# Prompt attention on one core: the values of a pair move between the second head's scores and its transposes

## The chip, the cores and the metric

The kernel runs on one NeuronCore of one Trainium2 chip. The metric is the device time of one execution in microseconds (us); the kernel before was timed three times, and the median of these runs is the number to compare with.

## What is computed

One inference step of a one-layer decoder with two groups of attention heads, for a prompt of 1024 positions and for eight short samples. The change touches the attention of the prompt alone. Cut to what matters there:

```python
def attend_block(t_pos, q_n, gates, q_f, cq, kw, vw, w_pos, kc, vc, c_end, ovl, ksb, vsb, kf, vf, ck, rel_bias):
    ...
    lc = jnp.einsum('bqgrd,bcgd->bgrqc', qg, kc).astype(jnp.float32) * scale + t5_bias_2d(dist_c, rel_bias)
    pc = masked_softmax(lc, dist_c >= 0)
    o_c = jnp.einsum('bgrqc,bcgd->bqgrd', pc.astype(vc.dtype), vc)
    ...
    ls = jnp.einsum('bqgrd,bgqmd->bgrqm', qg, ks_sel).astype(jnp.float32) * scale + bias_s.astype(jnp.float32)
    ps = masked_softmax(ls, (dist_s >= 0)[:, :, None])
    o_s = jnp.einsum('bgrqm,bgqmd->bqgrd', ps.astype(vs_sel.dtype), vs_sel)
    ...
    lw = jnp.einsum('bqgrd,bkgd->bgrqk', qg, kw).astype(jnp.float32) * scale + t5_bias_2d(dist_w, rel_bias)
    pw = masked_softmax(lw, valid_w)
    o_w = jnp.einsum('bgrqk,bkgd->bqgrd', pw.astype(vw.dtype), vw)
    ...
    lf = jnp.einsum('bqhd,bkhd->bhqk', q_f, kf).astype(jnp.float32) * scale + decay
    pf = masked_softmax(lf, k_pos[None, :] <= t_pos[:, None])
    o_f = jnp.einsum('bhqk,bkhd->bqhd', pf.astype(vf.dtype), vf).reshape(B, Q, FOX_HEADS * HEAD_DIM)
```

## The kernel before

The program has five stages one after the other: projections, the samples' attention, the prompt's attention (`build_c`, L1911 on), the output projection, and the feed-forward network. `build_c` is the stage of the change. In the profile its scores of the causal blocks start at 582 us and its last instruction ends at 957 us.

**Units, pairs, macros.** A unit is one softmax of 128 queries of one head (`unit_table`, L1626). Its kind is cmp, slc, win or fox. Two units, the two heads e = 0 and 1, make a pair `p`. For each of four head pairs hp and each of eight query tiles m there is a macro of three pairs: slc m, win m, fox m. The keys of a unit are n tiles of 128: n = m + 1 for slc, at most 5 for win, and 8 - m for fox, which takes its query tiles from the other end. One more pair, cmp of the next hp, stands between macro 4 and macro 5 of the first three head pairs. So there are 96 pairs with values and four of kind cmp.

**The way of a unit.** TensorE computes its scores into a slot of PSUM (`scores`, L2011; L2044 and L2045, both of type fp32r with 128-column weights). VectorE adds the bias and takes the maximum (`peak`, L2241). ScalarE takes the exponent (`exponent`, L2117, L2129) and counts `exp_done`. TensorE turns the probabilities in blocks of 128 x 128 (`turn`, L2048, L2053, fp32) into one of three banks of a ring, four blocks to an entry. ScalarE copies the entries out (`copies`, L2139), but VectorE copies the second entry of head 1 (L2289). At last TensorE multiplies the turned probabilities with the values (`values`, L2056, L2073 and L2080): fp32 matmuls on two halves of the array's columns, 64 wide each, one for either head, so that their weights have a shape that no other step of the loop has. An fp32 value product stands in the trace as two matmuls, so a pair of n tiles shows 4n of them, and slc pairs four more for cmp.

**Slots.** Four banks of PSUM hold scores. A unit with more than four tiles takes two banks, another one takes one (`slot_table`, L1707). Before it writes, `scores(u)` waits until the exponent of the unit that had its banks is done (L2102). For 50 of the second heads that is the unit two before, so the second head of the preceding pair; for the others it is an older one.

**Rounds.** Each engine has its order written out as a loop over rounds p. TensorE's is:

```python
for p in ROUNDS:
    for e in range(2):
        for u in pair_of(p + 1)[e:e + 1]:
            if SLOT_BEFORE[u] is not None:
                pe.wait_ge(exp_done, SLOT_BEFORE[u] + 1)
            scores(u)
        for u in pair_of(p)[e:e + 1]:
            pe.wait_ge(exp_done, u + 1)
            turn(u)
    if p - 2 in ENDS:
        natural(ENDS[p - 2])
    if p - 3 in ENDS:
        mix(ENDS[p - 3])
    if 0 <= p - 1 < NP:
        values(p - 1)
```

Written with S for scores, T for transposes, V for values and the head's number behind, a round is S0 T0 S1 T1 V, and its S belong to pair p + 1, its T to p, its V to p - 1. Four transposes of the finished macro (`natural`, L2084, L2088) stand ahead of V in a round of a win pair, two more (`mix`, L2091, L2095 and L2096) in that of a fox pair. Values of a cmp pair do nothing.

ScalarE's round (L2146 on) is: copies of head 0 of pair p, exponent of head 0 of p + 1, copies of head 1 of p, then in the round of a slc pair (or of cmp behind macro 4) the copy of the finished macro's sums `outT` (L2166), which waits until V of that round is done, and then the exponent of head 1 of p + 1. An engine works through its list in this order.

Of the kernel before, what the change touches and what calls it, by code (L numbers as in the profile page):

```python
# [1638 lines left out]
NP = NU // 2  # L1639
# [12 lines left out]
def key_tiles(m, kind):  # L1652

    if kind == "cmp":
        return 0, 4
    i = q_tile(m, kind)
    lo = max(0, i - WIN // P) if kind == "win" else 0
    return lo, i + 1 - lo
# [86 lines left out]
def pair_of(p):  # L1745

    return [2 * p, 2 * p + 1] if 0 <= p < NP else []
# [104 lines left out]
def fox_loads(hp):  # L1852

    return 128 * (hp // 2 + 1)
# [56 lines left out]
def build_c(nc, a, o, c, env, mixT, low, w_o, w_o_loaded, squares):  # L1911
# [13 lines left out]
    with ctx:  # L1925
# [33 lines left out]
        def query_of(macro, of):  # L1959
            hp, m = divmod(macro, QT)  # L1960
            if of == "nsa":
                return q_nsa[:, (hp + 1) % 2, :, m * P:(m + 1) * P], high_odd[:, 0] if macro % 2 else high_nsa
            i = q_tile(m, "fox")
            return q_fox[:, hp % 2, :, i * P:(i + 1) * P], high_odd[:, 1] if macro % 2 else high_fox

        def slot_of(u):
            hp, m, kind, e = UNITS[u]
            n = key_tiles(m, kind)[1] * P
            at = 512 * SLOT_BANK[u] + (512 - n // 2 if kind == "cmp" or n > 512 else 0)
            return slots[:, at:at + n]  # L1970
# [17 lines left out]
        with nc.Block() as block:  # L1988
# [19 lines left out]
            def _(pe):  # L2008
                pe.wait_ge(filled, 2)

                def scores(u):  # L2011
                    hp, m, kind, e = UNITS[u]
                    g = hp // 2
                    lo, n = key_tiles(m, kind)
                    slot = slots[:, 512 * SLOT_BANK[u]:]
                    if kind == "cmp":
                        if e == 0:
                            if hp == 0:
                                pe.wait_ge(kv_loaded, 192)
                            else:  # L2020
                                pe.wait_ge(q_loaded[hp % 2], 64 * ((hp + 1) // 2))
                        for j in range(4):
                            for par in range(2):
                                i = QT - 1 - 2 * j - par
                                part = slice(par * DH, (par + 1) * DH)
                                last = nc.tensor.matmul(slot[:, 256 + par * 256 + j * DH:256 + par * 256 + (j + 1) * DH],
                                                        q_nsa[part, (hp + 1) % 2, e, i * P:(i + 1) * P].bitcast(F32), k_cmp[part, g, :], start=True, stop=True)
                        last.then_inc(scored, 1)
                        return
                    if kind == "fox":  # L2030
                        if m == 0 and e == 0:
                            pe.wait_ge(fox_loaded[hp % 2], fox_loads(hp))
                        k = k_fox[:, hp % 2, e, :]
                    else:
                        k = (k_slc if kind == "slc" else k_win)[:, g, :]
                    of = "fox" if kind == "fox" else "nsa"
                    q_low, q_high = query_of(hp * QT + m, of)
                    if e == 0:
                        POOL.wait(pe, ("low", of, hp * QT + m))
                    dst = slot_of(u)  # L2040
                    w = n * P // 2 if n > 4 else n * P
                    for at in range(0, n * P, w):
                        keys = k[:, lo * P + at:lo * P + at + w]
                        nc.tensor.matmul(dst[:, at:at + w], q_high[:, e, :], keys, start=True, stop=False)  # L2044
                        last = nc.tensor.matmul(dst[:, at:at + w], q_low[:, e, :], keys, start=False, stop=True)  # L2045
                    last.then_inc(scored, 1)

                def turn(u):  # L2048
                    for g in entries_of(u):
                        _, at, n = ENTRIES[g]  # L2050
                        wait_place(pe, ("turn", g))
                        for j in range(n):
                            last = nc.tensor.transpose(place(("turn", g))[:, j * P:(j + 1) * P], probs[:, u % 4, (at + j) * P:(at + j + 1) * P], ident[:, :])  # L2053
                        last.then_inc(turned, 1)
# [43 lines left out]
# [3 lines that stand above are left out]
                            if SLOT_BEFORE[u] is not None:  # L2101
                                pe.wait_ge(exp_done, SLOT_BEFORE[u] + 1)  # L2102
                            scores(u)
                        for u in pair_of(p)[e:e + 1]:
                            pe.wait_ge(exp_done, u + 1)
                            turn(u)
                    if p - 2 in ENDS:
                        natural(ENDS[p - 2])
                    if p - 3 in ENDS:
                        mix(ENDS[p - 3])  # L2110
                    if 0 <= p - 1 < NP:
                        values(p - 1)

            @block.scalar
            def _(act):

                def exponent(u):  # L2117
                    hp, m, kind, e = UNITS[u]
                    n = key_tiles(m, kind)[1] * P
                    act.wait_ge(max_done, u + 1)  # L2120
                    if u >= 4:
                        act.wait_ge(turned, entries_of(u - 4)[-1] + 1)
                        if UNITS[u - 4][2] == "cmp":
                            STAT.wait(act, ("total", u - 4))
                    if kind == "cmp":
                        nc.scalar.activation(probs[:, u % 4, 0:n], slot_of(u), ACT.Exp).then_inc(exp_done, 1)
                    else:
                        at = 2 * KINDS.index(kind) + e
                        nc.scalar.activation(probs[:, u % 4, 0:n], slot_of(u), ACT.Exp, bias=neg_max[:, u % 4:u % 4 + 1], scale=-1.0 if turned_over(u) else 1.0,  # L2129
                                             accum_out=denom[:, m % 2, at:at + 1]).then_inc(exp_done, 1)  # L2130

                def copy(g):
                    u, at, n = ENTRIES[g]
                    hp, m, kind, e = UNITS[u]
                    act.wait_ge(turned, g + 1)
                    if u >= 4 and kind != "cmp" and UNITS[u - 4][2] != "cmp":
                        act.wait_ge(summed, summed_through((u - 4) // 2))
                    dst = cmpT[:, hp % 2, e, 0:n * P] if kind == "cmp" else probsT[:, u % 4, at * P:(at + n) * P]
                    nc.scalar.copy(dst, place(("turn", g))[:, 0:n * P]).then_inc(copied["A"], 1)  # L2139

                def copies(u):
                    for g in entries_of(u):
                        if ENTRY_ON[g] == "A":
                            copy(g)

                for p in ROUNDS:  # L2146
                    if p - 4 in ENDS:
                        macro = ENDS[p - 4]
                        hp, m = divmod(macro, QT)
                        src = place(("mix", macro))  # L2150
                        CLOSE_PE.wait(act, ("mix", macro))
                        nc.scalar.copy(mixT[:, hp, m * P:(m + 1) * P], src[:, 0:P])
                        i = q_tile(m, "fox")
                        CLOSE_ACT.done(nc.scalar.copy(mixT[:, H // 2 + hp, i * P:(i + 1) * P], src[:, P:2 * P]), ("mix", macro))
                    for u in pair_of(p)[:1]:
                        copies(u)
                    for u in pair_of(p + 1)[:1]:
                        exponent(u)
                    for u in pair_of(p)[1:]:
                        copies(u)  # L2160
                    if p - 1 in ENDS:
                        macro = ENDS[p - 1]
                        act.wait_ge(summed, summed_through(last_pair(macro)))
                        if macro:
                            CLOSE_PE.wait(act, ("natural", macro - 1))
                        CLOSE_ACT.done(nc.scalar.copy(outT[:, :, :].rearrange("p k n -> p (k n)"), outs), ("out", macro))  # L2166
                    for u in pair_of(p + 1)[1:]:
                        exponent(u)

# [1257 lines left out]
```

## Time and profile before

| | |
|---|---|
| median of three runs | 1823.34 us |
| lowest and highest | 1818.98 and 1825.59 us |
| time of the profiled execution | 1820.88 us |
| span of its instructions | 1819.2 us |
| busy over the span: PE (TensorE), DVE (VectorE), ACT (ScalarE) | 95%, 55%, 40% |
| mean granted TensorE clock | 0.98 |
| prompt attention, 582 to 957 us | 375 us |

The span runs from the first to the last instruction; 1.7 us of the execution's time lie outside of it. Matmuls are pipelined: one begins before the other's shown end, and their ends are modelled. So how long a run of matmuls holds the engine is read from start to start here. PE is the matmul row and PEld the row of weight loads. "idle before <-releaser" names what ended an engine's wait.

### The profile page before, as it was taken

The numbers are of one execution on the slowest core, as the hardware profiler recorded it, in microseconds if no ns is written. First come the engines' busy times: TensorE is split into PE (matmuls) and PEld (weight loads), VectorE is DVE, ScalarE is ACT, GpSimd is POOL, SyncE is SP. The second block draws the span as 40 slices with busy tenths as digits, with TensorE's granted clock in tenths as the row PEclk, the third lists the DMA queues.
The fourth block names the chain that finished last, engine by engine and source line by source line (L and its number), as shares of the span: only waits on it lengthen the run. The fifth ranks groups of instructions, "written<-read, shape, count | busy, mean of one in ns | idle before, by whom it ended". The sixth has DMA issues, their size and how long they took to land. (4 is left out here: it accounts for less than half of the span.)

```text
span 1819.2 us, 35393 instructions
## 1 busy us (share of the span) xinstructions
PE 1722.9 (95%) x13557; PEld 1577.7 (87%) x13557; DVE 1007.6 (55%) x1891; ACT 723.6 (40%) x1439; POOL 300.9 (17%) x629
## 2 busy tenths in 40 slices
PE   8999999799895999999998999999999999999998
PEld 7999998676573888888886879999999999999998
DVE  4533332124353666667665567766656664666665
ACT  5111010222231778676775642233333333344343
POOL 3000024410502434453530000000000000000000
PEclk9999999899996999999998999999999999999998
DMA  5548876645999103030202232222222225131112
GB/s 147 183 131 192 227 226 117 205 135 177 299 347 266 63 1 106 1 105 2 94 1 74 90 122 83 72 83 85 80 71 71 82 96 203 65 132 44 47 47 102
DMA packets 145682, 212.63 MB, mean 117 GB/s; under 512 B 23850, under 2 KB 102105, under 8 KB 145459
## 3 DMA queue, kind: packets, MB, share of 16 engines
q1 hardware_dynamic: 113714, 143.36, 24.8%
q0 software_dynamic: 16480, 52.41, 9.5%
q10 hardware_dynamic: 15328, 14.72, 3.3%
q8 instruction: 103, 1.69, 0.4%
q14 instruction: 57, 0.46, 0.1%
HBM read 163.11 MB, written 51.49 MB: 118 GB/s over the span
## 5 line engine op out<-in xcount | busy, mean ns | idle before, releaser
L191 PE MATMUL psum<-h_parts,down_hi 128*128 128x352 f32 x528 | 171.6, 325 | 5.9 <-DVE h_parts L3277 4.3
L191 PE MATMUL psum<-x_hi,w_hi 128*128 128x352 f32 x528 | 170.7, 323 | 1.4 <-issue 1.3
L192 PE MATMUL psum<-h_parts,down_hi 128*128 128x352 f32 x528 | 170.5, 323 | 0.0
L193 PE MATMUL psum<-h_parts,down_lo 128*128 128x352 f32 x528 | 170.4, 323 | 0.0
L192 PE MATMUL psum<-x_lo,w_hi 128*128 128x352 f32 x528 | 170.4, 323 | 0.0
L193 PE MATMUL psum<-x_hi,w_lo 128*128 128x352 f32 x528 | 170.3, 323 | 0.0
L191 PE MATMUL psum<-hf_hi,op_hi 128*128 128x264 f32 x576 | 163.5, 284 | 0.6 <-DVE silu L3258 0.6
L193 PE MATMUL psum<-hf_hi,op_lo 128*128 128x264 f32 x576 | 163.5, 284 | 0.0
L192 PE MATMUL psum<-hf_lo,op_hi 128*128 128x264 f32 x576 | 163.3, 284 | 0.0
L2129 ACT ACTIVATE probs<-psum,neg_max 128x640 f32<-128x640 f32 (+7 forms) x192 | 139.7, 728 | 20.0 <-DVE neg_max L2269 10.6
L2053 PE MATMUL psum<-ident,probs 128*128 128x128 f32 x848 | 129.1, 277 | 5.2 <-ACT probs L2129 4.0
L2139 ACT COPY probsT<-psum 128x512 f32<-128x512 f32 (+3 forms) x240 | 110.8, 484 | 54.6 <-PE psum L2053 53.1
L191 PE MATMUL psum<-t_hi,op_hi 128*128 128x264 f32 x432 | 123.0, 285 | 0.0
L193 PE MATMUL psum<-t_hi,op_lo 128*128 128x264 f32 x432 | 122.6, 284 | 0.0
L192 PE MATMUL psum<-t_lo,op_hi 128*128 128x264 f32 x432 | 122.5, 284 | 0.0
L2053 PEld LDWEIGHTS psum<-ident,probs 128*128 128x128 f32 x848 | 102.2, 141 | 18.7 <-ACT probs L2129 7.9
L734 DVE SCALAR_TENSOR_TENSOR z_stage<-psum,rstd 128x352 f32<-128x352 f32 x66 | 30.4, 516 | 158.2 <-PE psum L193 147.2
L191 PEld LDWEIGHTS psum<-hf_hi,op_hi 128*128 128x128 f32 x576 | 108.3, 188 | 0.8 <-DVE silu L3258 0.8
L193 PEld LDWEIGHTS psum<-hf_hi,op_lo 128*128 128x128 f32 x576 | 108.3, 188 | 0.0
L192 PEld LDWEIGHTS psum<-hf_lo,op_hi 128*128 128x128 f32 x576 | 108.3, 188 | 0.0
L191 PEld LDWEIGHTS psum<-h_parts,down_hi 128*128 128x128 f32 x528 | 99.1, 188 | 8.7 <-DVE h_parts L3277 6.3
L191 PEld LDWEIGHTS psum<-x_hi,w_hi 128*128 128x128 f32 x528 | 99.2, 188 | 2.8 <-issue 2.5
(455 smaller groups left out, 4258.0 us busy)
## 6 DMA issues: line engine op xcount, KB each, us to landing
fox_ring<-in_cache_fox_kv SPq DMA_DIRECT2D x128, 256.0 KB, 5.7
zT<-z_stage SPq DMA_DIRECT2D x22, 528.0 KB, 4.3
w_ring<-in_w_in POOLq DMA_DIRECT2D x22, 512.0 KB, 5.6
down_ring<-in_w_ffn_down SPq DMA_DIRECT2D x44, 256.0 KB, 2.7
raw<-in_w_ffn_gate SPq DMA_DIRECT2D x9, 1024.0 KB, 7.8
raw<-in_w_ffn_up SPq DMA_DIRECT2D x9, 1024.0 KB, 5.3
h_dram<-stage POOLq DMA_DIRECT2D x8, 1056.0 KB, 6.0
nsa_page<-in_cache_nsa_kv POOLq DMA_DIRECT2D x64, 128.0 KB, 6.2
```

Source lines behind the costliest of these rows:

```text
L191: nc.tensor.matmul(dst, w_hi, x_hi, start=start, stop=False, skip_group_check=onto)
L192: nc.tensor.matmul(dst, w_hi, x_lo, start=False, stop=False, skip_group_check=onto)
L193: return nc.tensor.matmul(dst, w_lo, x_hi, start=False, stop=stop, skip_group_check=onto)
L734: last = nc.vector.scalar_tensor_tensor(out=z_stage[:, s, tok], in0=bank[3 * s + b][:, 0:NB], scalar=scale, in1=rstd[:, tok], op0=ALU.mult ...
L2053: last = nc.tensor.transpose(place(("turn", g))[:, j * P:(j + 1) * P], probs[:, u % 4, (at + j) * P:(at + j + 1) * P], ident[:, :])
L2129: nc.scalar.activation(probs[:, u % 4, 0:n], slot_of(u), ACT.Exp, bias=neg_max[:, u % 4:u % 4 + 1], scale=-1.0 if turned_over(u) else 1.0, ...
L2139: nc.scalar.copy(dst, place(("turn", g))[:, 0:n * P]).then_inc(copied["A"], 1)
```

## The change

On TensorE, `values(p - 1)` stands after the scores of head 1 of pair p + 1 and ahead of the transposes of head 1 of pair p, where it was the last step of the round. A round is S0 T0 S1 V T1 then. On ScalarE, the copy of `outT` stands ahead of the copies of head 1, where it stood behind them. VectorE, GpSimd and SyncE keep their lists, and no instruction is added or taken away. The diff:

```diff
@@ build_c, @block.tensor
                             if SLOT_BEFORE[u] is not None:
                                 pe.wait_ge(exp_done, SLOT_BEFORE[u] + 1)
                             scores(u)
+                        if e == 1 and 0 <= p - 1 < NP:
+                            values(p - 1)
                         for u in pair_of(p)[e:e + 1]:
                             pe.wait_ge(exp_done, u + 1)
                             turn(u)
@@
                         natural(ENDS[p - 2])
                     if p - 3 in ENDS:
                         mix(ENDS[p - 3])
-                    if 0 <= p - 1 < NP:
-                        values(p - 1)
@@ build_c, @block.scalar
                         copies(u)
                     for u in pair_of(p + 1)[:1]:
                         exponent(u)
-                    for u in pair_of(p)[1:]:
-                        copies(u)
                     if p - 1 in ENDS:
                         macro = ENDS[p - 1]
                         act.wait_ge(summed, summed_through(last_pair(macro)))
                         if macro:
                             CLOSE_PE.wait(act, ("natural", macro - 1))
                         CLOSE_ACT.done(nc.scalar.copy(outT[:, :, :].rearrange("p k n -> p (k n)"), outs), ("out", macro))
+                    for u in pair_of(p)[1:]:
+                        copies(u)
                     for u in pair_of(p + 1)[1:]:
                         exponent(u)
```

TensorE's list, before, in the round of slc 6 (S of win 6, T of slc 6, V of fox 5) and the beginning of the next one:

```order
L2044 MATMUL psum<-k_win,high_nsa 128x320
L2045 MATMUL psum<-k_win,q_nsa 128x320
L2053 MATMUL psum<-ident,probs 128x128 x7
L2080 MATMUL psum<-probsT,v_fox 64x128 x6
L2044 MATMUL psum<-k_parts,high_fox 128x256
L2045 MATMUL psum<-k_parts,q_parts 128x256
L2053 MATMUL psum<-ident,probs 128x128 x5
```

The same place in the changed kernel:

```order
L2044 MATMUL psum<-k_win,high_nsa 128x320
L2045 MATMUL psum<-k_win,q_nsa 128x320
L2080 MATMUL psum<-probsT,v_fox 64x128 x6
L2053 MATMUL psum<-ident,probs 128x128 x7
L2044 MATMUL psum<-k_parts,high_fox 128x256
L2045 MATMUL psum<-k_parts,q_parts 128x256
L2053 MATMUL psum<-ident,probs 128x128 x5
```

The values now follow scores (fp32r) and precede transposes (fp32), where they followed transposes and preceded scores. (Their number is that of the program; the trace shows two for each.)

ScalarE's list, before, in the same round (exponent of win 6 head 0, copy of slc 6 head 1, `outT`, exponent of win 6 head 1):

```order
L2129 ACTIVATE probs,denom<-psum,neg_max 128x640
L2139 COPY probsT<-psum 128x512
L2166 COPY outT<-psum 128x512
L2129 ACTIVATE probs,denom<-psum,neg_max 128x640
L2139 COPY probsT<-psum 128x512
```

And in the changed kernel:

```order
L2129 ACTIVATE probs,denom<-psum,neg_max 128x640
L2164 COPY outT<-psum 128x512
L2139 COPY probsT<-psum 128x512
L2129 ACTIVATE probs,denom<-psum,neg_max 128x640
L2139 COPY probsT<-psum 128x512
```

The copy of `outT` has moved ahead of the copy of head 1's turned probabilities. In the rounds without it, two of three, ScalarE's list is as it was.

## Rows read from the trace of the kernel before

**Rows 1.** Busy time by stretch: prompt attention; us, busy PE, PEld, DVE, ACT, POOL, clock, DMA.
```profile
582.00:957.00 375.00, 362.17 (x3471) 305.82 (x3471) 250.20 (x895) 273.61 (x732) 162.12 (x389) 0.99 0.17 51
```

**Rows 2.** Who waited for whom, 582 to 957 us: total, times, longest.
```profile
ACT outT L2166 <- PE psum L2080: 15.3, 25, 1.4
PEld psum L2044 <- ACT probs L2129: 12.1, 38, 0.8
```

**Rows 3.** Timeline, TensorE, two rounds of macro 4, then fox 7's values: start, us, engine, line, operation.
```profile
720.29 0.41 PE L2044 MATMUL psum<-k_win,high_nsa 128*128 128x320 f32 x1
...
720.98 0.71 PE L2053 MATMUL psum<-ident,probs 128*128 128x128 f32 x5
721.45 0.39 PE L2044 MATMUL psum<-k_win,high_nsa 128*128 128x320 f32 x1
...
722.11 0.71 PE L2053 MATMUL psum<-ident,probs 128*128 128x128 f32 x5
722.75 1.31 PE L2080 MATMUL psum<-probsT,v_fox 128*64 128x128 f32 x20
...
723.99 0.50 PE L2044 MATMUL psum<-k_parts,high_fox 128*128 128x512 f32 x1
...
773.80 0.44 PE L2080 MATMUL psum<-probsT,v_fox 128*64 128x128 f32 x4
...
774.16 0.50 PE L2044 MATMUL psum<-k_parts,high_fox 128*128 128x512 f32 x1
```

**Rows 4.** Timeline, TensorE, the first transposes behind a pause, in two narrow windows.
```profile
754.84 0.33 PE L2053 MATMUL psum<-ident,probs 128*128 128x128 f32 x1 [0.26 <-ACT probs L2129]
...
755.01 0.38 PE L2053 MATMUL psum<-ident,probs 128*128 128x128 f32 x2
```

**Rows 5.** Timeline, the waits of T1 of win 6 and of win 7.
```profile
753.41 0.59 ACT L2166 COPY outT<-psum 128x512 f32<-128x512 f32 x1 [0.27 <-PE psum L2080]
753.90 0.80 ACT L2129 ACTIVATE probs<-psum,neg_max 128x640 f32<-128x640 f32 x1
...
754.31 0.28 PE L2045 MATMUL psum<-k_parts,q_parts 128*128 128x256 f32 x1
...
755.58 0.63 PE L2088 MATMUL psum<-ident,outT 128*128 128x128 f32 x4
...
767.31 0.80 PE L2053 MATMUL psum<-ident,probs 128*128 128x128 f32 x5 [0.35 <-ACT probs L2129]
```

**Rows 6.** Timeline, S1 of fox 3 waits for the exponent of win 3.
```profile
712.37 0.59 ACT L2166 COPY outT<-psum 128x512 f32<-128x512 f32 x1 [0.57 <-PE psum L2080]
712.85 0.69 ACT L2129 ACTIVATE probs<-psum,neg_max 128x512 f32<-128x512 f32 x1
...
712.95 0.60 PE L2053 MATMUL psum<-ident,probs 128*128 128x128 f32 x4
713.69 0.41 PE L2044 MATMUL psum<-k_parts,high_odd 128*128 128x320 f32 x1
```

**Rows 7.** Timeline, TensorE and ScalarE up to S1 of win 6.
```profile
747.93 0.49 PE L2053 MATMUL psum<-ident,probs 128*128 128x128 f32 x3
...
749.60 0.41 PE L2044 MATMUL psum<-k_win,high_nsa 128*128 128x320 f32 x1
...
750.29 0.93 PE L2053 MATMUL psum<-ident,probs 128*128 128x128 f32 x7
750.97 0.39 PE L2044 MATMUL psum<-k_win,high_nsa 128*128 128x320 f32 x1
...
748.38 1.01 ACT L2129 ACTIVATE probs<-psum,neg_max 128x896 f32<-128x896 f32 x1 [0.58 <-DVE neg_max L2280]
...
749.38 0.47 ACT L2139 COPY probsT<-psum 128x384 f32<-128x384 f32 x1
749.74 1.02 ACT L2129 ACTIVATE probs<-psum,neg_max 128x896 f32<-128x896 f32 x1
```

**Rows 8.** Timeline, the copy behind T0 of slc 4, which waited for nothing else.
```profile
721.62 0.76 ACT L2139 COPY probsT<-psum 128x512 f32<-128x512 f32 x2 [0.55 <-PE psum L2053]
```

**Rows 9.** Groups of instructions by line and shape, ScalarE, 600 to 945 us: busy, mean ns, idle before.
```profile
L2129 ACT ACTIVATE probs<-psum,neg_max 128x640 f32<-128x640 f32 x46 | 36.9, 801 | 2.9 <-DVE neg_max L2280 2.6
L2129 ACT ACTIVATE probs<-psum,neg_max 128x384 f32<-128x384 f32 x24 | 14.3, 596 | 0.2
```

## The prediction

> **What bounds the kernel now.** I read the busy time of the stage first, then who waited for whom, and then the timeline, since the change neither adds nor removes an instruction and only waits and neighbours can change. In its 375 us TensorE is busy for 362, ScalarE for 274 and VectorE for 250 [rows 1]. TensorE is the bound; a reorder can give back some of its idle 13 us and whatever the modelled ends hide. ScalarE waits 15.3 us for values ahead of the copy of `outT`, and the score of a second head waits 12.1 us for exponents [rows 2]. The first wait feeds the second: where values end late, `outT` is copied late, the exponent behind it in ScalarE's list is late, and TensorE waits. I read this from start to start, because shown ends overlap.
>
> **What the change does not touch.** The scores, their maxima and the exponents of head 0 keep their places. In a steady round the way from S0 to the next S0 holds the same five steps. So waits that end on head 0's exponent or on the maxima stay: those around the cmp pair, about 2.5 us for each of three head pairs by my reading of the starts, are costed at nothing in both kernels, since VectorE's list sets them.
>
> **Part 1, the neighbours of the values.** Before, values stand between transposes and scores. V with 20 matmuls takes 1.24 us up to the next score and V with 4 takes 0.36 [rows 3]; that is 0.055 for each matmul, and 0.15 more for the visit. The five transposes ahead take 0.64, though five take 5 x 0.11 = 0.55 [rows 3]: 0.09 lost. (0.11 is the step of transposes, from x3 with 0.49 to x7 with 0.93 [rows 7].) The first head's score behind values takes 0.69 up to its transposes, the second head's, behind transposes, 1.13 less 0.55, so 0.58 [rows 3]: 0.11 lost. A visit costs 0.09 + 0.15 + 0.11 = 0.35 us.
>
> After the change values stand between scores and transposes. That has no row. For the entry I take the same 0.09 + 0.15. For the exit the nearest rows are transposes that start behind a pause: their second one comes 0.17 behind the first instead of 0.11 [rows 4], so 0.06 lost where a score loses 0.11. The visit costs 0.30, and 0.05 is won. 96 pairs have values, and 93 of them are followed by scores of slc, win or fox (three by a cmp pair): 93 x 0.05 = **4.7 us won**. The bounds: nothing won, if transposes lose 0.11 as well; and 93 x 0.11 = 10 us dearer than this if values behind fp32r scores lose once more what a score loses behind values.
>
> The nearest rows say that a change of the weights' width costs time twice in a round, before and after alike. The Trainium skill ("TensorEngine Tiling (Array Packing)", section Key Properties) has a rule for it: a change of tiling mode drains the engine. By that rule alone both orders have two drains a round and Part 1 is worth nothing; the sum would be 4.7 us higher.
>
> **Part 2, the waits that go.** In macros 6 and 7, T1 of the win pair waits for the exponent behind `outT`. For win 6, `outT` starts at 753.41, the exponent at 753.90 and takes 0.80; the score ahead is through 0.11 after 754.31, at 754.42 [rows 5], and T1 starts at 754.84 [rows 4]: 0.42. Its five transposes and the step to `natural` take 0.74 instead of 0.55 [rows 4, 5], because the ring's copies wait behind the same exponent: 0.19. Win 7 has 0.52 and 0.19 (T1 at 767.31 [rows 5], by the same reading). Win 4 has 0.15 ahead of `natural`. After the change `outT` is copied while T1 of slc runs, V comes between S1 and T1, and T1 of win has over 1 us to spare. All of it goes: 0.42 + 0.19 + 0.52 + 0.19 + 0.15 = 1.47 us a head pair. Next late there is nothing on T1: the scores are.
>
> **Part 3, the waits that come.** T1 now ends the round. Behind it on ScalarE's list stand its copy and then the exponent of head 1, and in 50 rounds the next S1 needs the banks of just this exponent. Before, V lay in between; now only T1, S0 and T0 do. Counted from the start of T1:
>
> ScalarE: the copy starts 0.64 after four transposes begin (720.98 [rows 3] to 721.62 [rows 8]), 0.70 with the first load behind values, and 0.11 less for each block fewer. A copy of 512 columns holds ScalarE 0.48 (712.37 to 712.85 [rows 6]), one of 384 0.36 [rows 7], and I take 0.25 and 0.15 below. The exponent takes 0.80 for 640 columns and 0.10 a tile more or less [rows 9]. TensorE starts 0.15 after its end (712.85 + 0.69 to 713.69 [rows 6]).
>
> TensorE: 0.06 for the load, 0.11 for each block of T1 and T0 and of the four or two transposes at the round's end, 0.115 a tile for S0 (0.58 for five), less 0.09, by which a score starts ahead of the transposes' end (750.29 + 7 x 0.11 = 751.06 against 750.97 [rows 7]).
>
> The widest case is S1 of win 6: ScalarE 0.59 + 0.36 + 1.02 + 0.15 = 2.12, TensorE 0.06 + 10 x 0.11 + 0.58 - 0.09 = 1.65, a wait of 0.47. The trace has slack there now: the copy was held to 749.38 by head 0's exponent, and still S1 waited for nothing [rows 7]. The same sum gives win 4: 2.13 - 1.87 = 0.26, slc 4: 0.15, win 7: 0.14, slc 6: 0.05, and none for cmp and slc 7. Together 1.07 a head pair.
>
> S1 of fox 0 to fox 3 waits already: for fox 3 0.39 (713.69 against 712.95 + 0.44 - 0.09 [rows 6]), with fox 0 to 2 0.98. After the change `outT` comes 0.12 after T1's start and keeps ScalarE to 0.60, then copy and exponent follow. The sums give fox 3: 2.02 - 1.43 = 0.59, and 0.39, 0.30 and 0.18 for fox 2, 1 and 0: 1.46, so 0.48 more than now. `outT` is earlier, but the copy it has overtaken takes its place ahead of the exponent.
>
> Waits that come: 1.07 + 0.48 = 1.55 a head pair, against 1.47 that go: for four head pairs **0.3 us lost**.
>
> **Other edits.** VectorE's copies come later by V, but values of the same pair come only after two more scores, about 1.9 us; with that cover gone it would cost the copy, 0.3 us. `natural` now ends just ahead of S0, so weighing and copy (0.7 + 0.3) delay one maximum by some 0.3; this is head 0's, which has slack.
>
> **The sum** against the profiled execution, 1820.9 us, is -4.7 + 0.3 = -4.4, so 1816.5. That execution lies 2.5 under the median of the runs; against the median of 1823.3 the sum is **1818.9 us**, and I take 1819.
>
> **Rivals.**
> First, slower: ScalarE's chain closes into a loop. T1, copy, exponent, S1, V and T1 again; a round cannot be shorter than the loop. Against it speaks that my sums leave 0.0 to 0.47 of wait at 13 places of a head pair. For it: seven of these are within 0.2 of the edge, and rows show copies held 0.5 us and more by head 0's exponent (748.38 + 1.01 against a score ahead [rows 7]). If the chain is 0.35 longer than I take at all 50 places, 17.5 us are added: 1836.5. From 0.27 on it decides for slower by more than 0.5%. The Trainium skill ("TensorE: Matmul & The Clock Gate", section on the 16 sub-arrays) calls ScalarE's queue strictly first in, first out, which is what lets a waiting copy hold back a ready exponent.
>
> Second, faster: the chain is shorter than I take, no wait comes, and those of fox 0 to 3 (0.98) go too: 4 x (1.47 + 0.98) + 4.7 = 14.5, so 1808.8. For it speaks that `outT` is off ScalarE's way earlier; against it that each duration has a row.
>
> Third, no change: the exit from values costs the same to transposes as to scores, and waits trade evenly: 1823.3 + 0.3 = 1823.6.
>
> Fourth: values behind fp32r scores cost 0.11 more: 1818.9 + 10.2 = 1829.1, within 0.5% too.
>
> **The numbers.** A measurement of this kernel tells 0.5%, 9.1 us, from no change. Forecast 0.32, first rival 0.20, second 0.22, third 0.17, fourth 0.09. Faster by over 0.5% (below 1814.2) is the second rival and a little of the forecast's edge: 0.24. Slower (above 1832.5) is the first and a little of the fourth: 0.22. The rest is 0.54. The bounds are 1808.8 below; above, the fourth rival and 0.15 at 13 x 4 places, 7.8 us more: 1837. The range leaves the outer part of the first two rivals out: 1810 to 1833.
>
> **What would show it.** In the profile after: the wait of S1 (L2044) for ScalarE's exponent grows from 12 to some 14 to 20 us, and its places are win 6, fox 3 and win 4; that of T1 (L2053) for L2129 nearly goes, and so does ScalarE's wait for L2080 ahead of `outT`, of which less than 5 us stay. ScalarE's wait for L2053 ahead of copies grows by a third or more. The first two transposes behind values lie 0.17 apart, the first score behind transposes is short. The stage ends some 4 us earlier. The forecast is wrong if S1 waits in most of the 50 rounds, or if a visit of values comes to 0.35 or more.

## The result and the profile after

| | before | after |
|---|---|---|
| median (runs) | 1823.28 us (20) | 1826.53 us (20) |
| lowest and highest | 1818.89 and 1827.72 | 1823.64 and 1830.81 |
| first to last copy of `outT`, from the rows below | 355.0 us | 357.9 us |

The ratio is 1.0019 [1.0011, 1.0027]: the change makes the kernel slower by 0.2%, some 3.3 us. That is under the 0.5% called no change and inside the range, but it has the other sign than the forecast, which wanted 4.4 us off.

The work is the same. The page's line of busy times after, and then the stretch of prompt attention, to be held against [rows 1]:

```profile
PE 1724.7 (94%) x13557; PEld 1574.7 (86%) x13557; DVE 1007.2 (55%) x1891; ACT 728.2 (40%) x1439; POOL 300.6 (16%) x629
```

```profile
582.00:957.00 375.00, 358.95 (x3439) 298.60 (x3439) 250.28 (x897) 276.90 (x730) 158.88 (x379) 0.98 0.18 53
```

The two profiled executions differ by more than the medians, since the stage begins 3.2 us later in the second. Rows of one operation in the kernel before, with the shortest, median and longest ns, the first and the last start and the shapes: the exponents of the first kind of unit, and the copies of `outT`.

```profile
L2126 ACT ACTIVATE probs<-psum x8: 597/597/597, 578.3 to 827.0; 128x512 f32<-128x512 f32 x8
...
L2166 ACT COPY outT<-psum x32: 585/587/598, 598.4 to 953.4; 128x512 f32<-128x512 f32 x32
```

The same of the kernel after:

```profile
L2126 ACT ACTIVATE probs<-psum x8: 597/597/598, 581.5 to 832.3; 128x512 f32<-128x512 f32 x8
...
L2164 ACT COPY outT<-psum x32: 586/587/641, 601.8 to 959.7; 128x512 f32<-128x512 f32 x32
```

32 copies stand 355.0 us apart from first to last before and 357.9 after. These 2.9 us are the stage's own loss, near the 3.3 us of the medians; the 3.2 us ahead of the stage lie where both kernels have the same lists. This distance is used as "the stage" below.

Who waited for whom after (582 to 962 us: total, times, longest), for [rows 2]:

```profile
ACT probsT L2139 <- PE psum L2053: 49.7, 60, 2.0
DVE weighed L2315 <- PE psum L2088: 42.3, 26, 3.6
DVE probsT L2289 <- PE psum L2053: 22.3, 32, 1.8
PEld psum L2044 <- ACT probs L2129: 14.9, 34, 0.7
ACT outT L2164 <- PE psum L2080: 11.9, 20, 1.0
PEld psum L2053 <- ACT probs L2129: 3.8, 12, 1.7
```

Four of these in the kernel before, which [rows 2] leave out:

```profile
ACT probsT L2139 <- PE psum L2053: 53.1, 48, 2.6
...
DVE weighed L2315 <- PE psum L2088: 14.7, 14, 4.3
...
PEld psum L2053 <- ACT probs L2129: 7.9, 18, 1.6
...
DVE probsT L2289 <- PE psum L2053: 2.0, 4, 0.8
```

Two of the waits that the prediction named moved as it said: S1's for exponents went from 12.1 to 14.9 us, T1's fell from 7.9 to 3.8. Two did not: ScalarE's wait for values ahead of `outT` fell from 15.3 to 11.9 us, where less than 5 were to stay, and its wait for transposes ahead of copies fell from 53.1 to 49.7, where it was to grow by a third. What the prediction did not name moved most. VectorE's wait for `natural` (L2088) ahead of the weighing went from 14.7 to 42.3 us, and its wait for T1 ahead of its copy from 2.0 to 22.3. VectorE is busy for only 250 of 375 us, so waits there cost nothing by themselves; the question is what stood behind them in its list.

### The profile page after: what moved, and what is told of

It reads as the page before. It is cut to its first block and busy times, and to the rows that moved or that the text cites. A ratio compares the mean times of both kernels' runs of the same rounds, so it can differ in the third digit from the quotient of the medians.

```text
span 1825.2 us, 35393 instructions
## 1 busy us (share of the span) xinstructions
PE 1724.7 (94%) x13557; PEld 1574.7 (86%) x13557; DVE 1007.2 (55%) x1891; ACT 728.2 (40%) x1439; POOL 300.6 (16%) x629
## 5 line engine op out<-in xcount | busy, mean ns | idle before, releaser
L2053 PE MATMUL psum<-ident,probs 128*128 128x128 f32 x848 | 134.2, 283 | 3.1 <-ACT probs L2129 1.5
L2139 ACT COPY probsT<-psum 128x512 f32<-128x512 f32 (+3 forms) x240 | 112.4, 492 | 51.3 <-PE psum L2053 49.7
L2053 PEld LDWEIGHTS psum<-ident,probs 128*128 128x128 f32 x848 | 95.9, 141 | 28.8 <-issue 18.9
```

## Place by place

From start to start, mean of the second and third head pair, in us for one head pair (worked out from the timeline; the last two lines as far as they are apart). "Ring" is a wait inside T1 for a bank of the ring. Beside S0 of win 1 and S0 of slc 0 the wait lies behind that score, ahead of T0:

| place | before | after | forecast after |
|---|---|---|---|
| T1 and ring of win 6 / win 7, T1 of win 4 | 0.61 / 0.71 / 0.15 | 0.00 / 0.00 / 0.00 | 0 |
| S1 of win 6, win 4, slc 4, slc 6, win 7 | 0.00 | 0.46, 0.24, 0.14, 0.03, 0.00 | 0.47, 0.26, 0.15, 0.05, 0.14 |
| S1 of fox 3, 2, 1 | 0.39, 0.28, 0.17 | 0.58, 0.37, 0.27 | 0.59, 0.39, 0.30 |
| S1 of fox 0 | 0.14 | 0.45 | 0.18 |
| V behind it and the next S0 | 0.35 | 0.00 | 0.35 |
| S0 of win 7, with V ahead of it | 0.06 | 0.54 | as before |
| V of win 7 | 0.00 | 0.55 | 0 |
| S0 of win 1 | 0.00 | 0.22 | 0 |
| S0 of slc 0, S1 of slc 5, fox 7, win 5 | 0 | 0.19, 0.21, 0.10, 0.06 more | as before |

From one head pair's copy of `outT` to the next one's it takes 92.87 us before and 93.54 after: 0.67 more, where the forecast had 1.1 less. The lower four lines come to 1.8 us, which is the size of that miss; two smaller misses of Parts 1 and 3, told below, nearly cancel.

Three places in the timeline show the table. First the visit of values (kernel after, TensorE, round of slc 3):

```profile
713.99 0.47 PE L2044 MATMUL psum<-k_win,high_odd 128*128 128x512 f32 x1
714.31 0.39 PE L2045 MATMUL psum<-k_win,q_nsa 128*128 128x512 f32 x1
714.62 1.53 PE L2080 MATMUL psum<-probsT,v_fox 128*64 128x128 f32 x24
716.09 0.65 PE L2053 MATMUL psum<-ident,probs 128*128 128x128 f32 x4
716.50 0.39 PE L2044 MATMUL psum<-k_parts,high_odd 128*128 128x320 f32 x1
```

S1 holds TensorE from 713.99 to 714.62, 0.63; the same scores, with transposes behind them, took 0.55 before: 0.08 lost on entry, 0.09 forecast. V with 24 matmuls takes 1.47, which is 24 x 0.055 and 0.15. Four transposes up to S0 of fox 3 take 0.41; 4 x 0.11 less the 0.09 by which a score starts early would be 0.35: 0.06 lost, 0.06 forecast. A visit costs 0.29 to 0.32 by its neighbours, 0.35 to 0.37 before. By the Trainium skill's rule of a drain at each change of tiling mode ("TensorEngine Tiling (Array Packing)", Key Properties) both orders would have cost the same; the rows show time lost at each change, and how much depends on what stands next to it.

Over whole rounds the gain is smaller than 0.05. From one second head's score to the next one's, the seven rounds of a head pair in which neither order shows a wait changed by +0.02, +0.01 and -0.01 (those that end with `mix`), by -0.05 and -0.05 (with `natural`), and by -0.03 and -0.03 (with neither): 0.02 gained in mean. And `natural`, which now stands directly ahead of the scores of the cmp pair, takes 0.53 up to them, but 0.36 up to any other score.

Second, S1 of win 6, where the prediction put its widest wait (kernel after, TensorE and ScalarE):

```profile
754.93 0.93 PE L2053 MATMUL psum<-ident,probs 128*128 128x128 f32 x7
756.07 0.41 PE L2044 MATMUL psum<-k_win,high_nsa 128*128 128x320 f32 x1 [0.21 <-ACT probs L2129]
...
754.53 0.48 ACT L2139 COPY probsT<-psum 128x384 f32<-128x384 f32 x1 [0.41 <-PE psum L2053]
754.91 1.02 ACT L2129 ACTIVATE probs<-psum,neg_max 128x896 f32<-128x896 f32 x1
```

The exponent ends at 755.93, and the score starts 0.14 later. Behind seven transposes it would have started at 754.93 + 0.77 - 0.09 = 755.61: a wait of 0.46, for 0.47 forecast.

Third, the wait that nobody had asked for (kernel after, round of win 6):

```profile
762.08 0.60 PE L2088 MATMUL psum<-ident,outT 128*128 128x128 f32 x4
762.44 0.48 PE L2044 MATMUL psum<-k_slc,high_odd 128*128 128x512 f32 x1
762.82 0.69 DVE L2315 TENSOR_TENSOR weighed<-psum,factor 128x512 f32<-128x512 f32 x1 [2.39 <-PE psum L2088]
763.43 0.28 DVE L2289 COPY probsT<-psum 128x128 f32<-128x128 f32 x1
763.63 0.57 DVE L2326 CAST high_nsa<-q_nsa 128x256 fp32r<-128x256 f32 x1
764.12 0.42 DVE L2239 CUSTOM_DVE_ANT_0 psum<-psum,bias 128x256 f32<-128x256 f32 x1
765.64 1.11 ACT L2129 ACTIVATE probs<-psum,neg_max 128x1024 f32<-128x1024 f32 x1 [1.39 <-DVE neg_max L2280]
766.89 0.42 PE L2044 MATMUL psum<-k_win,high_odd 128*128 128x320 f32 x1 [0.30 <-ACT probs L2129]
```

The same round of the kernel before:

```profile
755.58 0.63 PE L2088 MATMUL psum<-ident,outT 128*128 128x128 f32 x4
756.34 0.69 DVE L2315 TENSOR_TENSOR weighed<-psum,factor 128x512 f32<-128x512 f32 x1 [0.98 <-PE psum L2088]
756.95 0.28 DVE L2289 COPY probsT<-psum 128x128 f32<-128x128 f32 x1
757.14 0.57 DVE L2326 CAST high_nsa<-q_nsa 128x256 fp32r<-128x256 f32 x1
758.03 0.50 PE L2044 MATMUL psum<-k_slc,high_odd 128*128 128x512 f32 x1
759.26 0.43 DVE L2239 CUSTOM_DVE_ANT_0 psum<-psum,bias 128x256 f32<-128x256 f32 x1 [1.55 <-PE psum L2045]
```

Before, S0 of slc 7 starts 2.45 us behind the start of `natural`, since V with 28 + 4 matmuls lies between, and VectorE is through with weighing, copy and cast 1.55 us before it can have its first bias. The bias comes 1.23 after the start of S0. After the change S0 starts 0.36 behind `natural`. By the same 1.23 the bias would start at 763.67; VectorE's list gets there at 764.12. The 0.45 pass on to the maximum, to the exponent of head 0, and to S0 of win 7, which needs that exponent's banks and starts 0.54 late. Those 1.55 us of VectorE's slack were not named in the prediction at all.

## The experiments

Two accounts stood against each other. By the first, theory A in the expectations where it has a letter, the loss comes through VectorE's list (weighing waits for `natural`, and copy and next maximum wait behind it). By its rival, it is ScalarE's chain of copy, exponent and S1, longer than forecast. Stages are first to last copy of `outT`. The kernels of one group ran on one chip beside the kernel before: 1824.1 us for pe_only, act_only, exp_first and nat_early, 1823.5 for nat_only, dve_copy_first and the two hybrids, 1822.7 for the other four. Every ratio is to the kernel before of the same group, with its 95% interval.

**pe_only and act_only: either half alone.** The first takes only the move of `values` (before: `for e ...: S, T; natural; mix; values`), the second only ScalarE's edit:

```diff
+                        if e == 1 and 0 <= p - 1 < NP:
+                            values(p - 1)
...
-                    if 0 <= p - 1 < NP:
-                        values(p - 1)
```

```diff
-                    for u in pair_of(p)[1:]:
-                        copies(u)
                     if p - 1 in ENDS:
...
+                    for u in pair_of(p)[1:]:
+                        copies(u)
```

> TensorE's half of the change alone: ScalarE copies outT behind the copies of head 1, as before. Theory of the chain: in the eight slc rounds of a head pair the exponent of head 1 comes 0.5 us later than in the changed kernel, since outT (0.48) no longer fits ahead of the copy, and S1 of fox 1 to 3 and of win 5 wait that much longer: +2 us a head pair, 1834. If outT's place on ScalarE does not matter: 1826.5.

> ScalarE's half of the change alone: values stay last in the round. outT waits for V at the round's end, and now the copy of head 1 stands behind it, so the exponent of head 1 is 0.48 later in eight rounds of a head pair. If these waits decide (S1 of fox 0 to 3, of win 5, T1 of win 4, 6 and 7): +0.48 x 6 to 8 x 4, so 1835 to 1839. If ScalarE's order is free there: 1823.3.

pe_only: 1829.39 us, 1.0034 [1.0018, 1.005], stage 362.2. act_only: 1833.68, 1.006 [1.0045, 1.0076], stage 366.1. Either half alone is worse than both. In pe_only the exponent stands behind a copy and `outT`:

```profile
715.26 0.59 ACT L2139 COPY probsT<-psum 128x512 f32<-128x512 f32 x1 [1.16 <-PE psum L2053]
715.74 0.59 ACT L2166 COPY outT<-psum 128x512 f32<-128x512 f32 x1
716.22 0.70 ACT L2129 ACTIVATE probs<-psum,neg_max 128x512 f32<-128x512 f32 x1
...
717.07 0.42 PE L2044 MATMUL psum<-k_parts,high_odd 128*128 128x320 f32 x1 [0.81 <-ACT probs L2129]
```

S1 of fox 3 waits 1.06, the 0.48 of one copy more than after. S1 of fox 1, fox 2 and win 5 waits 0.36 to 0.48 more too, 1.8 a head pair with fox 3, but some of it is given back: the step behind `natural` in the round of slc 5 waits 0.48 less. So 1829.4 came out for 1834. In act_only S1 of fox 3 waits 0.87 and T0 of win 6 and win 7 0.53 and 0.59, less in sum than expected; why it stayed under was not followed further.

**exp_first: after, with the exponent of head 1 ahead of `outT` and of the copies.**

```diff
                     for u in pair_of(p + 1)[:1]:
                         exponent(u)
+                    for u in pair_of(p + 1)[1:]:
+                        exponent(u)
...
-                    for u in pair_of(p + 1)[1:]:
-                        exponent(u)
```

> The changed kernel, with head 1's exponent of pair p + 1 ahead of outT and of the copies of head 1 of pair p on ScalarE. Theory of the chain: the waits at S1 of win 6, win 4, slc 4 and fox 0 to 3 (2.5 us a head pair in the changed kernel's trace) go, those behind natural stay: 1826.5 - 10 = 1816.5. Rival: the copies come later by an exponent (0.4 to 1.1 us), and values and the ring wait for them instead: 1826 or more, with waits of V (L2080, L2073) for L2139 well over 8 us.

1845.19 us, 1.012 [1.0102, 1.0137]. Its waits:

```profile
PEld psum L2053 <- ACT probsT L2139: 19.3, 26, 1.2
PE psum L2053 <- ACT probsT L2139: 19.1, 38, 1.1
...
PEld psum L2044 <- ACT probs L2129: 6.7, 11, 1.0
```

S1's wait for exponents fell from 14.9 to 6.7, so that chain is what Part 3 took it for. But now T waits for the banks of the ring, whose copies stand behind the exponent; in the changed kernel this wait was 0.2 us in each of the two rows. The order copy, exponent is the better one.

**nat_early: after, with `natural` and `mix` between S1 and V** (the table of the ring's order likewise), to give VectorE back the time of V:

```diff
+                        if e == 1 and p - 2 in ENDS:
+                            natural(ENDS[p - 2])
+                        if e == 1 and p - 3 in ENDS:
+                            mix(ENDS[p - 3])
                         if e == 1 and 0 <= p - 1 < NP:
                             values(p - 1)
...
-                    if p - 2 in ENDS:
-                        natural(ENDS[p - 2])
-                    if p - 3 in ENDS:
-                        mix(ENDS[p - 3])
```

> The changed kernel, with the transposes of the finished macro (natural, mix) moved from the end of the round to between S1 and V, and their places in the ring with them. Theory A (VectorE held by natural): in the changed kernel VectorE's wait for natural (L2315 for L2088) grew from 14.7 to 42.3 us, and behind it stand the copy of head 1's second entry and the next maximum of head 0; with natural early this wait falls under 20 us, and the waits at S0 of win 7 (0.54), V of win 7 (0.55), and around S0 of slc 0 and win 1 (0.2 each) go, 1.4 us a head pair. But natural and mix no longer lie between T1 and the next S1, so the waits at S1 of slc 4, win 4, slc 7 and win 7 grow by some 0.85 us together. Net -0.55 a head pair: 1824, between 1823 and 1825. Theory B (ScalarE's chain T1, copy, exponent, S1 is all of the loss): 1826.5 + 3.4 = 1830.

1858.75 us, 1.0189 [1.0173, 1.0205], stage 391.7: a miss by some 30 us. Its waits:

```profile
PEld psum L2055 <- ACT probs L2131: 31.7, 39, 1.5
PE psum L2055 <- ACT mixT L2156: 24.0, 27, 1.2
```

`mix` too has an entry in the ring of three banks, and ScalarE copies it where it did. T1's entries now come behind that of `mix`, and wait for a copy that stands late in ScalarE's list. It says nothing about either account.

**nat_only: the same with `natural` alone moved.**

> The changed kernel, with natural alone moved from the end of the round to between S1 and V (its place in the ring with it); mix stays. In the run that moved both, transposes waited 30.6 us for ScalarE's mixT copies, whose bank now came round too early, so that run did not test VectorE's part; this one does. Theory A (natural directly ahead of S0 holds VectorE): VectorE's wait for L2088 falls from 42.3 to under 20 us; the waits at S0 of win 7 and V of win 7 (0.54 and 0.55) and those around slc 0 and win 1 (0.2 each) go, 1.4 us a head pair; S1 of slc 4 waits 0.57 instead of 0.14 and S1 of slc 7 some 0.15, since natural no longer lies ahead of them. Net -0.8 to -0.9 a head pair: 1823. If A is wrong: those waits stay and 1828 comes out.

1825.97 us, 1.0017 [1.0007, 1.0027], stage 359.7. VectorE's wait for `natural` went (42.3 to 3.1 us), and with it the named waits: S0 of win 7 0.54 to 0, V of win 7 0.55 to 0.15, S0 of win 1 0.22 to 0.04. S1 of slc 4 came to 0.58, since T1 begins later (0.57 forecast). S1 of win 7 now waits 0.13, which Part 3 had at 0.14. S1 of slc 1 (0.52) came unforeseen, and some 0.2 between S1 of win 5 and S1 of fox 5. The account holds at its places; the total does not move, and against the 1823 expected the run is a miss. S0 of slc 0 lost its 0.2 too.

**dve_copy_first: after, VectorE's copy ahead of the weighing.**

```diff
-                    if p - 2 in ENDS:
-                        weigh(ENDS[p - 2])
                     for u in pair_of(p):
                         for g in entries_of(u):
                             if ENTRY_ON[g] == "V":
                                 copy(g)
+                    if p - 2 in ENDS:
+                        weigh(ENDS[p - 2])
```

> The changed kernel, with VectorE copying head 1's second entry ahead of weighing instead of behind it. Theory A in its second half: V of win 7 (0.55) waits for this copy, which stands behind weighing, which waits for natural. The copy is ready after T1, so V's wait goes; the maximum of head 0 still stands behind weighing, so S0 of win 7 still waits 0.54. -0.5 us a head pair, 1824.5. If V of win 7 waits for something else: 1826.5.

1820.22 us, 0.999 [0.9978, 1.0002], stage 353.4: 6.3 us faster than the changed kernel by the medians, which are of different groups, 5.3 by the two ratios, whose intervals do not touch, and 4.5 by the stage. Its waits:

```profile
DVE probsT L2289 <- PE psum L2053: 47.3, 45, 2.5
...
DVE weighed L2315 <- PE psum L2088: 12.3, 13, 3.1
```

V of win 7 waits 0.00 (0.55), S0 of win 1 0.04 (0.22), S0 of win 7 0.14 (0.54). That is 1.1 us a head pair through one swap on an engine that is busy for two thirds of the stage. One more wait went, 0.57 for the ring at T0 of win 5, which the kernel before has too; so up to 2.3 of the 6.3 us are not the change's cause undone. 0.28 and 0.25 came at T1 of fox 7 and behind the `natural` after it.

**before_dve: the same swap in the kernel before.**

> The kernel before, with VectorE copying head 1's second entry ahead of weighing. The changed kernel gained 6.3 us by this edit (1826.5 to 1820.2). In the kernel before natural has V behind it and VectorE is not held; only T0 of win 5 waits for this copy (0.60 a head pair): 0.57 x 3 head pairs with a cmp pair, about 1.7 us, 1821.6. If the edit is worth the same in any order: 1817.

1825.45 us, 1.0011 [0.9998, 1.0023]: no gain. T0 of win 5 went from 0.60 to 0.03, but 0.17 came behind it ahead of T1, and 0.67 ahead of `mix`. So the swap is worth nothing by itself: it pays where `natural` stands directly ahead of S0.

**hybrid and hybrid_no_nat: `values` early in the rounds of win 4, 6 and 7 alone**, where T1 waited. In hybrid `natural` comes early there too; in hybrid_no_nat it stands at the round's end, so directly ahead of S0, as in the change. ScalarE's list is that of before.

```diff
+EARLY_VALUES = (('win', 4), ('win', 6), ('win', 7))
...
+                        if e == 1 and p - 2 in ENDS and values_early(p):
+                            natural(ENDS[p - 2])
+                        if e == 1 and 0 <= p - 1 < NP and values_early(p):
+                            values(p - 1)
```

> The kernel before, with natural and then values between S1 and T1 in the rounds of win 4, 6 and 7 alone, where T1 waited; all other rounds and ScalarE's list as before. The waits of 0.42 and 0.19 (win 6), 0.52 and 0.19 (win 7) and 0.15 (win 4) go, and the places where ScalarE's chain made S1 wait keep their values behind T1; natural is early, so VectorE is not held. 1.47 us a head pair plus 3 x 0.05 for the neighbours: 6.5 us, 1817.5. By a theory in which every early V costs its win again later: 1823.

> The same with natural left at the end of the round, directly ahead of S0. Theory A: VectorE is held by weighing again in these rounds, and S0 of win 7 (0.5) and V of win 7 (0.55) wait: 1.0 of the 1.6 us a head pair is given back, 1821. If natural's place does not matter: as the run with natural early, 1817.5.

hybrid: 1820.19 us, 0.999 [0.998, 1.0], stage 353.1. hybrid_no_nat: 1829.78, 1.0039 [1.0025, 1.0052], stage 362.0. They differ in the place of `natural`, in TensorE's list and in the ring, in three rounds of a head pair, and by 9.6 us. The wait that sets them apart, in hybrid:

```profile
DVE weighed L2329 <- PE psum L2098: 3.7, 2, 3.1
```

and in hybrid_no_nat:

```profile
DVE weighed L2323 <- PE psum L2094: 28.0, 13, 2.7
```

This is the second witness against the rival: ScalarE's list is the same in both. The direction was expected; the size was nearly three times that. Two things in the trace of hybrid_no_nat that are not in that of hybrid tell why:

```profile
PE psum L2101 <- POOL o_sum L2230: 3.0, 4, 0.8
...
775.00:785.00 10.00, 10.00 (x64) 7.71 (x60) 4.49 (x13) 4.90 (x16) 3.35 (x8) 0.66 0.53 124
```

First, `mix` in the round of fox 7 waits for GpSimd's sum, which waits for the late weighing: 0.9 in each of the first three head pairs, so the late `natural` is passed on through a third engine. Second, the granted clock was 0.66 from 775 to 785 us (half for some 7 us of it, the lower of its two levels), where hybrid has 1.00. From S1 of slc 0 to S1 of slc 2 this head pair takes 22.23 us and the one before it 19.43, so 2.8 of the 8.9 us between the two stages are the clock. Some 6 are the place of `natural`.

hybrid itself lost part of its gain to a wait of 0.61 behind S1 of slc 0, where T1 of fox 7 waits for ScalarE's exponent; what makes that one late was not tried.

**hybrid_dve: hybrid with VectorE's copy ahead of the weighing.**

> Natural and values early in the rounds of win 4, 6 and 7 alone, and VectorE's copy ahead of weighing. The first was worth 3.3 us against the kernel before, the second takes the wait of T0 of win 5 (0.60) away, which the first left: 1820.2 - 1.7 = 1818.5. If the two take away the same wait: 1820.2.

1836.37 us, 1.0075 [1.0053, 1.0097], stage 365.5: 18 us off. The profiled execution is its fastest, 1828.12 us, so the trace shows about 10 of the 16 us that it lies over hybrid; for 3.4 us of its stage the granted clock was at half. The row that was not there in hybrid:

```profile
PE psum L2063 <- DVE weighed L2329: 9.9, 12, 1.5
```

`natural` uses a bank of the ring, and the weighing frees it. Where `natural` stands ahead of V and T1, the weighing now waits behind a copy that waits for T1, so by the lists the bank comes free a whole V later. VectorE's best order depends on TensorE's.

**before_nat_only: before, with `natural` alone between S1 and T1.**

> The kernel before, with natural alone between S1 and T1; values stay last. T1 of win 6 and win 7 waits 0.42 and 0.52 for ScalarE's exponent, and natural's 0.43 of work now lies in this wait: -0.4 each, -0.85 a head pair, 1820. VectorE gets natural earlier still. If natural's place only matters where S0 follows it directly: 1823.3.

1821.33 us, 0.9996 [0.9983, 1.001]. T1 of win 6 and win 7 waited 0.42 and 0.52 for an exponent behind S1. Now it waits 0.55 and 0.65 behind `natural`, for a copy:

```profile
754.46 0.74 PE L2055 MATMUL psum<-ident,probs 128*128 128x128 f32 x5 [0.39 <-ACT probsT L2141]
```

By the order of the ring `natural` has taken the bank that T1's first entry had, and T1 needs one that ScalarE copies out behind the exponent. The wait did not go, it found another cause. The expected 0.85 a head pair is not there: 1820 was forecast, and the interval includes no change.

**selective: `values` early in 16 of the 24 rounds of a head pair, VectorE's copy first, `natural` as before, ScalarE's list as before.** Late stay slc 0 to 3, slc 5, win 3, fox 3 and fox 5. The rounds were chosen from the places at which either order waited.

```diff
+EARLY_VALUES = (('win', 0), ('fox', 0), ('win', 1), ('fox', 1), ('win', 2), ('fox', 2), ('slc', 4), ...
...
+                        if e == 1 and 0 <= p - 1 < NP and values_early(p):
+                            values(p - 1)
```

> Values early in all rounds but those whose T1 is followed by a waiting S1: slc 0 to 3 and 5, win 3, fox 3 and 5; ScalarE's list as before; VectorE's copy ahead of weighing; natural where it was. Against the changed kernel with the copy ahead of weighing (1820.2) the waits at S1 of win 6 (0.46), win 4 (0.23), slc 4 (0.14) and fox 1 to 3 (0.1 to 0.2 each more than before) go, 1.2 us a head pair; 8 of 24 visits of values are the dearer ones again, 0.4: net -0.8, 1817. If the chain is not what these waits are: 1820.

1819.08 us (1813.31 to 1822.21, 12 runs), 0.9974 [0.996, 0.9988]. 1817 was expected. It is faster than before by 0.26%, and faster than the changed kernel, whose interval lies wholly above. Against dve_copy_first the intervals overlap; that the choice of rounds adds something to VectorE's order rests on one trace of each, 349.6 us of stage against 353.4. The copies of `outT` stand 349.6 us apart:

```profile
L2174 ACT COPY outT<-psum x32: 586/590/600, 598.1 to 947.7; 128x512 f32<-128x512 f32 x32
```

and its waits:

```profile
PEld psum L2050 <- ACT probs L2137: 10.5, 33, 0.8
...
DVE weighed L2323 <- PE psum L2094: 7.4, 9, 3.1
```

T1's gain of Part 2 is kept, S1 of win 6, win 4 and slc 4 waits for nothing and S1 of fox 1 to 3 as before (0.17 to 0.39), and VectorE's wait for `natural` is under that of the kernel before.

## Why the prediction was wrong in sign and right in most of its steps

**What the change does not touch**: "keep their places" was true of the lists and wrong of the times. This sentence sent me past VectorE, whose list stayed the same while what it waits for moved by a whole V.

**Part 1** holds at the neighbours and was too large in sum. The values' visit costs some 0.30 by the rows, for 0.35 before, as forecast, and the first two transposes behind values lie 0.17 apart, as forecast. But 0.05 a visit would be 1.2 us a head pair. What is left of the measured 0.67 when all waits of the table are taken out is 0.9 gained, 3.5 us in all for 4.7: rounds that end with `mix` gain nothing, and `natural` ahead of the cmp scores costs 0.17 more. The fourth rival (0.11 dearer) and the third (nothing won) both fall at the entry of 0.08 and the exit of 0.06.

**Part 2** holds: 1.47 us forecast, 1.47 by the starts.

**Part 3** holds at its places. S1 of win 6, win 4, slc 4, slc 6 and fox 1 to 3 are within 0.03 of their sums. Win 7 had 0.14 forecast and has none while S0 of win 7 waits; without that wait it has 0.13 (nat_only). Fox 0 was mis-sized (0.45 for 0.18), but the 0.35 that had been waited one step on went, so that it nets to nothing. In sum 1.2 us came, for 1.55 forecast. exp_first and pe_only show the chain for what it is: take the copy out, and the wait goes; put 0.48 in, and it grows by 0.48. The first rival, by which the chain closes at all 50 places (51 by the slot table), does not hold.

**Other edits** is the step that failed: "`natural` now ends just ahead of S0, so weighing and copy (0.7 + 0.3) delay one maximum by some 0.3; this is head 0's, which has slack". The delay is the right one (0.45 in the row above, for 0.3), the slack is not there. The maximum of slc 7's head 0 sets its exponent, and this exponent's banks are what S0 of win 7 waits for: 0.48 us a head pair. VectorE's own copy is late behind the same weighing, and V of win 7 waits for it: 0.55. (The prediction priced that copy, at 0.3, and took its cover of "two more scores, about 1.9 us" for enough; behind slc 0, with one tile, scores are far shorter.) S0 of win 1 adds 0.22. These 1.25 us a head pair, 5 us in all, turn the forecast of 4.4 off to about nothing. That VectorE's list is their cause is shown by dve_copy_first, where 1.1 of the 1.25 go with one swap on VectorE, and by hybrid and hybrid_no_nat, which differ in the place of `natural` and by some 6 us that are not the clock.

This step should have been done like Part 3: VectorE's list, from the end of `natural` through weighing, copy and cast to the next bias, against TensorE's way to that S0. The trace of the kernel before had what it takes: 1.55 us of idle time ahead of the bias, with a V of 1.9 us to be taken out from under it.

What stays open: S1 of slc 5, fox 7 and win 5 (0.4 us a head pair together) were not tried apart from the others. S0 of slc 0 (0.2) went in nat_only and stayed in dve_copy_first, so it hangs on the place of `natural` and not on VectorE's order; its cause was not tried further. In sum over the four head pairs: 4.4 us were to come off; Other edits put 5.0 on, these four places 2.2, and Part 1's shortfall 1.2, while Part 3's waits came out 1.4 smaller than forecast. That is 2.6 us of loss, against 2.9 in the stage.

## What to carry to other kernels

A long step on the engine that sets the pace is cover for the lists of all the others at once. Before it is moved, go through every engine's list at the place that it leaves, not only at the one to which it goes: what does each engine have to do between its last input from ahead of the step and its next from behind it, and is that shorter than what is left there?

Where engines work through fixed lists and hand a few banks of PSUM round, a wait that is taken away can come back one step on, or for another cause; here nat_only and before_dve lost waits at their places and gained nothing in sum, and in before_nat_only the same step waited for something else. The one variant that was faster than before beyond noise chose round by round, from the places at which either order waits, together with VectorE's copy ahead of the weighing.

## What the runs showed of the chip that I had not expected

The cost of going from matmuls with 128-column weights to 64-column ones and back depends on the neighbour: 0.15 us within, 0.08 to 0.09 on entry, and on exit 0.11 to an fp32r score but 0.06 to fp32 transposes.

A swap of two instructions of 0.69 and 0.28 us on VectorE, which is busy for 67% of the stage, moved the time by 6.3 us in one order of TensorE's list, by nothing in another (before_dve, 2.7 us with an interval that includes no change), and by 16 us the wrong way in a third (hybrid to hybrid_dve, 1820.19 and 1836.37, in groups whose kernels before differ by 0.8 us; 12.4 us by the stage).
